# Where the hi/lo weight splits and three small steps stand in a one-core decoder layer in fp32r

## What is computed

```
h = rmsnorm(x);  p = h @ w_in[l]            # q/k/v of 8 differential heads, q/k/v/gate of 4 gated linear heads
gk = log_sigmoid(gate_lr @ w2 + b2) / 16     # gates of the linear heads, then cumulated
p_diff = softmax(q0 k0) - lam * softmax(q1 k1);  o_da = rmsnorm(p_diff @ v)
o_gla = chunked gated linear attention;  y = concat(o_da, o_gla) @ w_out[l]
x = x + rmsnorm(y)
h = rmsnorm(x)
u = h @ w_up[l];  uc = conv_b + sum(conv_w[i] * shifted(u, i))     # causal, width 3
a, val = split(uc);  y = (silu(a) * val) @ w_down[l]
x = x + rmsnorm(y)                            # meta tokens dropped
```

## Time and profile before

| what | value |
|---|---|
| median of three executions | 1224.23 us |
| the profiled execution, time / span | 1221.97 / 1220.2 us |
| TensorE matmul busy | 1204.0 us (99%) |
| VectorE / ScalarE / POOL busy | 667.8 / 603.4 / 481.9 us |
| granted TensorE clock, mean | 0.998 |
| HBM read | 209.53 MB, 173 GB/s over the span |
| w_lo: POOL's L399 / VectorE's L399 | 190 x 2459 ns / 202 x 1323 ns |

### The profile page before, as it was taken

The page is one execution under the profiler, slowest core; times in us unless marked ns, Lnnn a source line. Parts: engine busy times, 40 slices in busy tenths (PEclk is TensorE's granted clock), DMA queues, the critical chain, the costliest instruction groups (busy, mean ns, idle before and its releaser), DMA issues.

```text
span 1220.2 us, 23725 instructions
## 1 busy us (share of the span) xinstructions
PE 1204.0 (99%) x8948; PEld 1144.4 (94%) x8948; DVE 667.8 (55%) x958; ACT 603.4 (49%) x908; POOL 481.9 (39%) x222
## 2 busy tenths in 40 slices
PE   9999999999999999999999999999999999999997
PEld 9899999999999999999999999999999988888885
DVE  7755545554465347756656656666666642232234
ACT  7444545355655447544444444444445544444444
POOL 0133333323344432344444444444444444444443
PEclk9999999999999999999999999999999999999999
DMA  9645455544445564565665655665665565655651
GB/s 330 199 141 167 138 158 142 156 122 134 139 142 183 178 191 146 164 187 169 195 185 163 195 184 170 191 186 173 189 181 180 186 198 187 200 193 190 195 167 69
DMA packets 175695, 212.31 MB, mean 174 GB/s; under 512 B 6688, under 2 KB 162720, under 8 KB 175520
## 3 DMA queue, kind: packets, MB, share of 16 engines
q1 hardware_dynamic: 175216, 210.32, 56.2%
q10 hardware_dynamic: 432, 1.34, 0.3%
HBM read 209.53 MB, written 2.10 MB: 173 GB/s over the span
## 4 chain that ended last, share of the span: by engine, by line
PE 92%; DVE 4%; ACT 1%; DMA 1%; issue 1%; SPq 0%; DVEq 0%; ACTq 0%
PE psum L415 68%; PE psum L1761 19%; PE psum L1405 1%; DVE w_lo L399 1%; DMA raw<-in_w_in 1%; DVE a_lo L1235 1%; DVE a_lo L945 1%; PE psum L1460 1%; PE psum L1570 1%; PE psum L1789 0%; PE psum L1486 0%; DVE psum L1243 0%; DVE xT L1251 0%; ACT w_hi L395 0%; PE psum L1588 0%
## 5 line engine op out<-in xcount | busy, mean ns | idle before, releaser
L399 POOL TENSOR_TENSOR w_lo<-raw,w_hi 128x1024 fp32r<-128x1024 f32 x190 | 467.2, 2459 | 716.7 <-ACT w_hi L395 716.7
L415 PE MATMUL psum<-a_hi,w_hi 128*128 128x258 f32 (+1 forms) x2360 | 674.0, 286 | 3.6 <-DVE a_lo L945 1.2
L415 PE MATMUL psum<-a_lo,w_hi 128*128 128x258 f32 (+1 forms) x2360 | 671.7, 285 | 0.0
L415 PE MATMUL psum<-a_hi,w_lo 128*128 128x258 f32 (+1 forms) x2360 | 669.5, 284 | 0.0
L395 ACT ACTIVATE w_hi<-raw 128x1024 fp32r<-128x1024 f32 x391 | 411.8, 1059 | 473.9 <-PE psum L415 345.2
L399 DVE TENSOR_TENSOR w_lo<-raw,w_hi 128x1024 fp32r<-128x1024 f32 x202 | 267.2, 1323 | 409.6 <-ACT w_hi L395 408.6
L415 PEld LDWEIGHTS psum<-a_hi,w_hi 128*128 128x128 f32 x2360 | 448.1, 190 | 10.2 <-issue 5.5
L415 PEld LDWEIGHTS psum<-a_lo,w_hi 128*128 128x128 f32 x2360 | 447.6, 190 | 0.0
L415 PEld LDWEIGHTS psum<-a_hi,w_lo 128*128 128x128 f32 x2360 | 446.2, 189 | 0.1
L1295 DVE SCALAR_TENSOR_TENSOR proj<-proj,par 128x256 f32<-128x256 f32 x88 | 112.2, 1275 | 38.8 <-ACT proj L812 38.8
L1761 PE MATMUL psum<-w_hi,a_hi 128*128 128x512 f32 x336 | 130.7, 389 | 0.0
(11 more groups left out here) (232 smaller groups left out, 619.3 us busy)
## 6 DMA issues: line engine op xcount, KB each, us to landing
raw<-in_w_up SPq DMA_DIRECT2D x176, 512.0 KB, 3.6
raw<-in_w_in SPq DMA_DIRECT2D x95, 512.0 KB, 4.2
raw<-in_w_down SPq DMA_DIRECT2D x88, 512.0 KB, 4.1
raw<-in_w_out SPq DMA_DIRECT2D x32, 512.0 KB, 3.9
xT<-in_features SPq DMA_DIRECT2D x3, 544.0 KB, 7.6
temp<-in_post_ffn_g ACTq DMA_DIRECT2D x1, 1024.0 KB, 4.5
out<-proj SPq DMA_DIRECT2D x2, 512.0 KB, 2.7
out<-proj SPq DMA_DIRECT2D x4, 256.0 KB, 2.9
```

The source lines that it names most:

```text
L399: eng.tensor_tensor(w_lo[:, j % SPLIT, :], raw[:, j, :], w_hi[:, j % SPLIT, :], ALU.subtract)\
L415: mm = pe.matmul(psum[:, bank + m, 0:t1 - t0], w[:, j % SPLIT, cols], a[:, k, t0:t1], start=(k == 0 and step == 0), stop=(k == KT - 1 and ...
```

## The change

Five edits, none of which changes a value. (1) ScalarE's Abs and Exp of the gates move from slot 11 to slot 10, its Ln from slot 12 to slot 11, VectorE's L1012 from slot 13 to slot 12. (2) ScalarE's w_hi of w_up's chunk 3 moves from behind the root (L786) to behind the second `up_hi`. (3) VectorE's w_lo of w_up's chunk 2 moves from the third round of the loop over feature tiles (L1269) to directly behind that of chunk 0, ahead of L1226. TensorE has two more filler calls: two matmuls between the two token sums, and three instead of two behind them. (4) The copy of rb2 is awaited by the chain's semaphore instead of one of its own. VectorE's w_lo of chunk 6 of w_up's second group moves from between the two evacuations of the first group to behind its gate. (5) The last four chunks of the second group go to banks 2, 3, with `up_chunk`'s wait for their evacuation, instead of banks 6, 7 with the waits for `nat_free` and `row_copied`.

```diff
@@ ScalarE, loop over slots, inside "if slot == LR_SLOT + 1"
                     act_e.wait_ge(par_ready, 1)
-                if slot == LR_SLOT + 2:
+
                     for hd in range(n_gla):
                         await_evacuated(act_e, ("gates", hd))
                     link(act_e.activation(az_all, z_all, ACT.Abs))
                     link(act_e.activation(az_all, az_all, ACT.Exp, scale=-1.0))
-                if slot == LR_SLOT + 3:
+                if slot == LR_SLOT + 2:
                     act_e.activation(az_all, az_all, ACT.Ln, bias=1.0).then_inc(soft_ready, 1)
@@ ScalarE, after the root of y
-            split_hi(act_e, OUT1 // RAW, 3)
...
             up_hi(0)
             up_hi(1)
+            split_hi(act_e, OUT1 // RAW, 3)
@@ VectorE, loop over slots
-                if slot == LR_SLOT + 4:
+                if slot == LR_SLOT + 3:
 
                     dve.wait_ge(soft_ready, 1)
@@ VectorE, end of w_out
             out_half(N_OUT - 1, 0)
-            split_lo(dve, OUT1 // RAW, 0)
+            split_ahead_out(N_OUT - 1, 1)
             dve.wait_ge(y_summed, 1 + KT // 2)
@@ VectorE, loop over feature tiles
                 up_lo(2 * g - 1)
-                if g == 2:
-                    split_lo(dve, OUT1 // RAW, 2)
                 if g == 4:
@@ VectorE, w_up's first groups
-            dve.tensor_copy(rb2[:], psum[:, NAT_BANK, 0:NQ]).then_inc(row_copied, 1)
-            dve.wait_ge(row_copied, 1)
+            link(dve.tensor_copy(rb2[:], psum[:, NAT_BANK, 0:NQ]))
             evacuate_up(0, 0, RAW - 1, u_sb_new=True)
-            split_ahead_up(1, 2)
             evacuate_up(0, 1, RAW)
             gate_up(0)
+            split_ahead_up(1, 2)
             evacuate_up(1, 0, 4, bank=Y2_BANK)
             split_ahead_up(1, 4)
             split_ahead_up(1, 6)
-            evacuate_up(1, 1, 8, bank=ROW_BANK)
+            evacuate_up(1, 1, 8)
@@ TensorE, token sums
             token_sums(0, y_acc[:, 0, :])
+            busy(Y2_BANK, 2)
             pe.wait_ge(y_squared, KT)
             token_sums(1, y_sq[:, 1, :]).then_inc(y_sums_full, 1)
-            busy(Y2_BANK, 2)
+            busy(Y2_BANK, 3)
@@ TensorE, w_up's second group
                 else:
-                    if j == 4:
-                        pe.wait_ge(nat_free, 8)
-                        pe.wait_ge(row_copied, 1)
-                    project_chunk(pe, OUT1 // RAW + 1, j, ROW_BANK, 0, NQ)
+                    up_chunk(1, j)
```

More of the change, by code:

```diff
@@ L364, in trunk @@
         nat_full, nat_free, nat_squared = sem("nat_full"), sem("nat_free"), sem("nat_squared")
-        row_copied = sem("row_copied")
         halo_summed, halo_full, x1_ms_ready, x1_root_made, x1_rstd_made, x1_row_full = (
```

## The result

The changed kernel takes 1232.76 us (median of 6 executions, 1231.89 to 1233.62), the kernel before 1223.23 us (6 executions, 1221.97 to 1226.35). The ratio is 1.0076, with a 95% interval of 1.0065 to 1.0087. The medians lie 9.5 us apart, where 3.9 were forecast, and 1232.76 us lies above the range, which ended at 1231.0. The profiled execution took 1233.57 us, with a span of 1231.8.

What follows compares the result with a forecast made beforehand. TensorE, busy 99% of the span, bounds the kernel, so other engines' edits count only where it waits. Terms 0.8+2.4+0.7=3.9 us on 1221.97 give 1225.9, plus 2.26 to the median: 1228.1 us (ratio 1.0032), range 1222.5 to 1231.

Steps and rivals of the forecast that it cites:

- the places named: TensorE standstills: about 2.6 us before the first probs_T, 1.6 near 460 to 462, 1.6 before w_up's chunk 6.
- Parts 2 and 3: From w_out to w_up, +2.4 us; w_up's second group, +0.7 us.
- Part 1: The gates (slots 10 to 13): scores' 1.84 us wait goes, probabilities come late; +0.76 us.
- its own bound of +1.3: At the gates: upper bound, if a further 0.5 us is lost in L1051's collision with POOL.
- The step that failed: At the gates: POOL's subtraction moves along with Exp, probabilities at 65.52 instead of 64.23, TensorE stands 2.6 us.
- The clock: Rival: TensorE's clock falls as standstills grow to 2.6 and 1.6 us; a 10 us stage at half pace costs 10; chance 0.03.
- Rival 1: At a_lo 1, VectorE takes the port before POOL: sum 2.9, total 1227.1 us; chance 0.15.
- The gain of w_lo 2's leaving the chain: Between w_out and w_up: VectorE's a_lo chain, relieved of w_lo 2, regains 1.1 us.
- Rivals 2, 3 and 4: Gates gain, 1226.3 us, chance 0.15; port holds nobody, 1221.9, chance 0.1; w_lo 6's delay reaches group three, 1229.5, chance 0.1.
- Rival 4's 1229.5: w_lo 6's lateness reaches group three's first chunks, +1.6, and the gates cost +1.3: sum 5.3, 1229.5 us; chance 0.1.

Runs made afterwards that it cites:

- experiment 2: Kernel before with only the gates' Abs, Exp and Ln a slot earlier on ScalarE, L1012 left behind the masks: 1224.34 us, ratio 0.9994.
- 3: Kernel before with the whole gates edit, and ScalarE's split 17 held until the first head's probabilities are made: 1224.00 us, ratio 0.9995.
- p1_only: Kernel before with the gates edit alone (Abs, Exp, Ln and L1012 one slot earlier): 1229.96 us, ratio 1.0040.
- before_again: Kernel before, unchanged, run once more for a second profile: 1225.83 us, one execution.
- p3_banks_only: Kernel before with the new banks and the chain's semaphore only, w_lo 6 at its old place: 1228.15 us, ratio 1.0023.
- experiments 6 and 11: Kernel before with part 2 but w_hi 3 unmoved: 1226.48 us; kernel before with gates early on ScalarE, split 17 held, w_lo 2 and third group's w_lo 0 moved: 1221.58 us.
- experiment 9: The same run as p3_banks_only: kernel before with new banks and the chain's semaphore, w_lo 6 at its old place: 1228.15 us, ratio 1.0023.

## Why the prediction missed

**The direction and the places were right; the size was not.** Three standstills at the places named, none at the scores, none at the third group. Parts 2 and 3 measured +2.6 and +0.7 against +2.4 and +0.7, by profiles; the near match of part 2 has luck in it, as 0.3 of its 2.6 belongs to the profile it is measured against, and by medians it is +2.0. Part 1 measured +5.8 against +0.76, and outside its own bound of +1.3.

**The step that failed is in part 1:** "the POOL subtraction that stretches L1051 (61.25) hangs on ScalarE's Exp and moves along: probabilities at 65.52". It does hang on Exp and did move along, from 61.25 to 63.18. Had it been alone, the pair would have taken 2.80 us as before and ended at 63.34+2.80=66.14 instead of 68.20, 2.06 earlier, and TensorE would have stood 3.0 us where I had said 2.6 (the masks were 0.64 later than worked out: 0.27 of it is start-up, and ScalarE's Abs began 0.43 behind the end of L999, at 49.98, where I had taken 0.05). What I didn't ask is what else moves along. ScalarE is through with Exp at 62.04 instead of 60.10, and TensorE is 1.6 us earlier in its chunks than before, 3.5 us further in all. So splits 18 and 19, which used to wait 1.01 and 1.83 us for TensorE, wait no longer: three splits run in one go (x3, 2.96 us), and the first and third of them are POOL's. The bound of "a further 0.5 us" took the same collision at another offset; one subtraction for each of the two instructions was a case I didn't count. It cost 2.06 us and, with the longer standstill, the clock. Experiments 2 (one collision, 2.78 us for the pair) and 3 (none, 0.78 us) show it from both sides.

**The clock: a rival priced by its own mechanism, but held for unlikely.** I gave it 0.03 on the strength of one profile that kept 2.4 GHz through 1.84 us. It fell in the kernel after (2.66 us), in p1_only, and behind that very 1.84 us in two of the seven profiles that have it (before_again and p3_banks_only). So the term that I left out of the sum was not a rare one. The price, 10 us for a stage of 10, wasn't met: it was 2.66 us for 6.8 at the lower level, and 1.2 to 1.6 for 3.4. Sum of part 1: 0.76+0.4+2.06+2.66=5.9, beside 5.8 measured.

**Part 2.** L1228 later by w_lo 2, the fillers at 0.44, POOL ahead of a_lo 1 by 0.07 us (465.35 beside 465.42, exactly the margin worked out) and a_lo 1 at 2.59 us: all as written. A margin of 0.07 us is thin: at a_lo 8 a smaller one came out both ways. Rival 1, that VectorE wins, did not come about in the profiles. The Trainium skill ("SBUF — State Buffer", Who interferes with whom) says that issue order, not the shape of the operation, decides who blocks; by that rule 465.35, 465.42 and the 2.59 agree. The gain of w_lo 2's leaving the chain was taken at 1.1 and was mostly a wait in another place (experiments 6 and 11: 0.15 on TensorE); in the kernel after TensorE was 2.6 late by the sums and the collision, so that this didn't show.

**Part 3.** w_lo 6 behind the gate, 1.60 us, and 0.93 back: as written, alone and in the whole. That the banks cost nothing because the evacuation goes first was right, and experiment 9 shows the price of it being otherwise.

**Rivals 2, 3 and 4** are out: the scores' 1.85 us were won but not kept; the port holds (0.78 against 2.78 against 4.86 us); nothing of w_lo 6 reached the third group. Rival 4's 1229.5 lay nearest to what was measured, but by luck: it put the growth in part 3 and 0.5 us of it in part 1. The forecast should have had a second subtraction as a case of its own, 2.06 on top of 1228.1, so 1230.2 us, and the clock on top of that.

**What stays open:** why the lower clock lasts 6.8 us in one profile and 3.4 in others behind a standstill of one size, the fall at 246.5 us, and why some runs had many more falls than others. Whether the parts add to each other is all but settled. By medians they cost 5.2, 2.0 and 0.6 us alone, 7.8 together. The whole's 9.5 is taken against a median of 1223.23 from six executions; against the 1224.67 to 1224.78 of the 23 to 26 beside the experiments it is 8.0 to 8.1, though not measured beside them.

## What to carry to other kernels

When an engine is made late at one instruction, list all that has become permitted behind it in the meantime: the queue is then released in one go, and a pair of instructions of which one used to meet a neighbour has both meet one. Price a collision for every instruction of the group and every one that the other engine has ready, not for one, and give a fall of the clock behind the standstill its own term. A small step moved "earlier" cost nothing here on the engine with slack (ScalarE: 1224.34 beside 1224.78 us) and cost 5.2 us together with the one that lands ahead of a chain (VectorE's masks); the two halves of such an edit are worth trying apart. And a single profile of the kernel before is one draw: here it was the faster one in three places (no fall, a_lo 8, w_up's pace).

## What the runs showed of the hardware that was not expected

- VectorE and POOL, both running back to back, stayed in step: having been held once by POOL, VectorE's next instruction again came just behind POOL's next (65.5 and 65.6 us), and was held for its whole length too, 4.86 us for 0.78 us of work. With a pause of 0.30 us on POOL (experiment 2) the second instruction got in ahead and took 0.49 us.
- The granted clock fell to the 1.2 GHz level behind standstills of 5.06, 5.09 and 2.15 us, and behind one of 1.84 us in two of seven profiles; in a further profile it fell with none ahead. Behind the seven standstills of 1.54 to 1.73 us at the places of the change it didn't. The stretches at the lower level were 6.8 us once (2.66 us lost) and 3.4 us in the others (1.2 to 1.6 us lost).
- Which of VectorE and POOL gets in first was decided by 0.01 to 0.07 us, and at a_lo 8 it came out one way in one profile and the other way in seven.
- At a granted clock of 1.00 throughout, w_up's matmuls took 0.1200 us each in some executions (three of the 14 profiles, of three kernels) and 0.1206 in the others, 2.1 us over the stage.
